# Which row of a step a token gets: ranks laid eight rows apart, in two mixture-of-experts stages

## The chip, the cores and the metric

The kernel runs on one core of one Trainium2 chip. The metric is device time in microseconds (us) of one execution. Median of three runs before the change: 1887.09 us (1879.42 to 1887.37).

## The reference, cut to what matters

Two transformer blocks over one sequence of 512 tokens with 1024 features, in float32. Each block mixes the tokens (attention and gated linear attention in the first, two attentions in the second) and then runs a mixture of experts. Only the latter is touched:

```python
# first block: 32 experts in 4 groups; each token takes the 2 best experts of its best group
hid = silu(h @ w_g[e]) * (h @ w_u[e]) * gate[:, e]      # w_g[e], w_u[e]: 1024 x 256
out = out + hid @ w_d[e]                                # w_d[e]: 256 x 1024
# second block: 64 experts in 8 groups; each token takes 6 experts out of its 4 best groups
xb = x_pad[tok]                                         # the tokens of expert e
hb = silu(xb @ w_exp_gate[e]) * (xb @ w_exp_up[e])
yb = (hb @ w_exp_down[e]) * g[:, None]
routed = segment_sum(yb, row_tok)                       # added back to each token's row
```

So 512 x 2 = 1024 (token, expert) pairs are computed in the first block and 512 x 6 = 3072 in the second. An expert's three weights are 1 MiB each, and all are read from HBM once: 96 MiB and 192 MiB.

## The kernel before, in words

Every expert stage works in steps of 128 rows, the partitions of an on-chip tile. A row of a step holds one token of one expert. A token's *rank* is its place among the tokens that chose the expert.

- First block, `paired_experts_stage`, 16 steps: expert `e` has rows 0 to 63 and expert `e + 8` rows 64 to 127.
- Second block, `sorted_experts_stage`, 39 steps. Experts 0 to 3 have a step each (WHOLE, 128 rows). The other sixty are sorted by their count on the chip; the ten largest get 128 rows each, the next fourteen 96 rows and share a step with one of the fourteen smallest in the other 32 (MIXED), and the twenty-two between pair up with 64 rows each (EVEN). `expert_steps` interleaves them.

For each step, VectorE compares each token's rank with a row of numbers, one for each row of the step (`onehot`, L1753 and L2083), TensorE multiplies this with the token numbers and gives a list: the token of each row, or a number past the end where a row has none. GpSimd issues an indirect DMA that gathers the listed rows of `h_scratch` (4 KB each) into the step's 128 rows (L1805, L2133), three steps ahead of their use. TensorE turns them (L1695, L2021), multiplies by gate and up weights (L1682, L2008), turns the hidden rows (L1670, L1996) and multiplies by the down weights (L1718, L2043). GpSimd then issues a second indirect DMA that adds the 128 result rows to the accumulator in HBM (`scatter_add`, L2329). Rows without a token are skipped by both.

Weights come by plain DMAs from SyncE's queue, 1 MiB each, over 128 partitions of 8 KB (L1608 and L1612 in the first block, L1554 to L1564 in the second). Their buffers are rings: in the first block the gate and up loads of pair p are issued once the gate and up products of pair p - 3 are done, the down loads of pair p - 1 once the down products of pair p - 3 are. SyncE issues in program order; an issue itself can take long when the queue is full. All DMAs, SyncE's and GpSimd's, run on the same 16 DMA engines.

The numbers that the ranks are compared with are, before, 0, 1, 2, ... (`K.iota`) in the first block and 1, 2, 3, ... (`order.places`, the last `held` of 1 to 128) in the second, where a slot with fewer rows has an offset added to its ranks. So rank n stands in row n of the expert's part of the step.

The routing and the ranks are made one stage earlier, in `output_and_ranks` of each block; VectorE there waits for the router's product before `vector(...)` (L1329).

Of the kernel before, what the change touches and what calls it, by code (L numbers as in the profile page):

```python
# [18 lines left out]
ALU = mybir.AluOpType  # L19
# [3 lines left out]
P = 128  # L23
S = 512
T = S // P
# [1152 lines left out]
def output_and_ranks(K, tag, preload, m, width, router, gate=None, gate_ready=None, vectors=(), gain=None,  # L1178
# [9 lines left out]
    load_router, load_next, scalar, vector = router  # L1188
# [6 lines left out]
    with nc.Block(no_gpsimd_drain=True) as block:  # L1195
# [101 lines left out]
        @block.vector  # L1297
        def _(dve):
            step = K.dve.on(dve)

            def add(u):
                j, t = divmod(u, T)
                x = K.x[:, t, 512 * j:512 * j + 512]
                dve.wait_ge(K.products, at_out[u])
                src = K.bank[u][:, :]
                if gate is not None:
                    step(dve.tensor_tensor(src, src, gate[:, 512 * j:512 * j + 512], ALU.mult))
                dve.tensor_tensor(x, x, src, ALU.add).then_inc(added, 1)

            weights.low(dve, 0)  # L1310
            weights.low(dve, 1)
            if gate is not None:
                dve.wait_ge(*gate_ready)
            for t in range(T):
                add(t)
            dve.wait_ge(*gain_ready)
            if scale is not None:
                step(dve.scalar_tensor_tensor(out=gain, in0=scale, scalar=1.0, in1=gain, op0=ALU.add, op1=ALU.mult))
            for t in range(T):
                add(T + t)  # L1320
                dve.wait_ge(std, t + 1)
                step(dve.reciprocal(rs[:, t:t + 1], sd[:, t:t + 1]))
                ins = dve.scalar_tensor_tensor(out=K.hr[:, t, :], in0=K.x[:, t, :], scalar=rs[:, t:t + 1], in1=gain,
                                               op0=ALU.mult, op1=ALU.mult)
                if shift is not None:
                    step(ins)
                    ins = dve.tensor_tensor(K.hr[:, t, :], K.hr[:, t, :], shift, ALU.add)
                ins.then_inc(normed, 1)
            dve.wait_ge(K.products, K.router_at)  # L1329
            vector(dve, step, K.bank[2][:, 0:T * width].rearrange("p (t n) -> p t n", t=T))  # L1330
            step(dve.tensor_copy(m.table[:, :, :, 1], m.gate))
            dve.tensor_copy(m.table[:, :, :, 0], K.token_id[:, :].unsqueeze(2).broadcast_to([P, T, E])).then_inc(chosen, 1)

            if shared:
                shared.vector(dve)
            for t in range(T):
                step(dve.memset(m.parts[:, t, :, 0], float(P * t - NO_TOKEN)))
            step(dve.tensor_scalar(m.parts[:, :, :, 1], K.token_id[:, 0:1].unsqueeze(2).broadcast_to([P, T, E]),
                                   float(NO_TOKEN), None, ALU.add))
            if order:  # L1340
                order.constants(dve, step)
                dve.wait_ge(K.products, at_rank[0])
                order.vector(dve, step)
                return
            step(dve.tensor_copy(m.parts[:, :, :, 2], m.gate))
            step(dve.tensor_tensor(m.rest, m.gate, m.parts[:, :, :, 2], ALU.subtract))
            step(dve.tensor_copy(m.parts[:, :, :, 3], m.rest))
            step(dve.tensor_tensor(m.rest, m.rest, m.parts[:, :, :, 3], ALU.subtract))
            step(dve.tensor_copy(m.parts[:, :, :, 4], m.rest))
            dve.wait_ge(K.products, at_rank[0])  # L1350

            step(dve.scalar_tensor_tensor(out=m.rank, in0=K.bank[3][:, 0:T * E].rearrange("p (t e) -> p t e", t=T),
                                          scalar=1.0, in1=m.chosen, op0=ALU.add, op1=ALU.mult))
            dve.tensor_scalar(m.rank, m.rank, -1.0, None, ALU.add).then_inc(tables, 1)
            dve.tensor_reduce(m.tiny[:, 0:1], K.bank[2][:, 0:E], AX.X, ALU.max).then_inc(tables, 1)
            dve.wait_ge(tables, 2)
            step(dve.tensor_copy(m.most, m.tiny[:, 0:1]))
# [50 lines left out]
QUARTER = P // 4  # L1408
# [16 lines left out]
    return steps  # L1425


def row_tiles(part):
    if part.stop - part.start in (QUARTER, 3 * QUARTER):
        return [slice(n, n + QUARTER) for n in range(part.start, part.stop, QUARTER)]  # L1430
    return [part]


class ExpertOrder:


    def __init__(self, K, m):
        s = K.sem
        self.K, self.m = K, m
        made, made_mm = s("order_tables_made"), s("order_products_made")  # L1440
        self.beats_ready, self.slots_ready, self.rank_ready, self.ids_ready, self.turned_copied = ((made, n) for n in range(1, 6))
        self.place_mm, self.ids_mm, self.turn_mm, self.slot_mm = ((made_mm, n) for n in range(1, 5))
        self.made, self.made_mm = made, made_mm
        f = K.heads
        self.key_base, self.key, self.beats, self.light, self.count = (f[:, 5120 + 64 * n:5184 + 64 * n] for n in range(5))
        self.junk, self.slots, self.turned = f[:, 5440:5568], f[:, 5568:5696], f[:, 5696:6208]
        self.own, self.beaten, self.slot, self.last, self.number = (f[:, 6208 + n:6209 + n] for n in range(5))
        self.places = K.small[:, 768:896]
        self.scatter_base = {EVEN: K.small[:, 896:897], MIXED: K.small[:, 897:898]}
        self.ids = K.small[0:1, 900:964].bitcast(I32)  # L1450
        flat = K.keep.rearrange("p t s -> p (t s)")
        self.both = flat[:, 512:1024].rearrange("p (t n) -> p t n", t=T)
        m.rank, m.gate = self.both[:, :, 0:64], self.both[:, :, 64:128]
        self.rank = m.chosen

    def constants(self, dve, step):
        K = self.K
        step(dve.tensor_scalar(self.key_base, K.iota[:, 0:64], -1.0, 63.0, ALU.mult, ALU.add))
        step(dve.tensor_scalar(self.key_base[:, 0:STATIC], K.iota[:, 0:STATIC], -FIXED, STATIC * FIXED, ALU.mult, ALU.add))
        step(dve.tensor_scalar(self.places, K.iota[:, :], 1.0, None, ALU.add))  # L1460
        step(dve.tensor_scalar(self.number, K.token_id[:, 0:1], float(NO_TOKEN), None, ALU.add))
        step(dve.tensor_scalar(self.last, self.number, 64.0, 64.0, ALU.is_ge, ALU.mult))
        step(dve.tensor_scalar(self.scatter_base[EVEN], self.last, float(S // 64), float(NO_TOKEN), ALU.mult, ALU.add))
        step(dve.tensor_scalar(self.own, self.number, float(3 * QUARTER), float(S), ALU.is_ge, ALU.mult))
        step(dve.tensor_scalar(self.scatter_base[MIXED], self.own, float(NO_TOKEN), None, ALU.add))
        step(dve.tensor_scalar(self.last, self.last, 63.0, None, ALU.add))
# [159 lines left out]
HALF = P // 2  # L1626


def paired_experts_stage(K, m, weights, next_vectors):
# [12 lines left out]
    onehot = f[:, 7680:8192].bitcast(BF16).rearrange("p (b t s) -> p b t s", b=2, t=T)  # L1642
# [17 lines left out]
    with nc.Block(no_gpsimd_drain=True) as block:  # L1660
# [64 lines left out]
        def _(dve):  # L1725
            for i in steps:
                if has(i, 0):
                    b, r = i % 2, i % 6
# [6 lines left out]
                if has(i, 1):  # L1735
                    b = (i + 1) % 2
# [4 lines left out]
                if has(i, 3):  # L1741
                    if i >= 3:
                        dve.wait_ge(scattered, 16 * (i - 2))
                    q = (i + 3) % 6
# [4 lines left out]
                if has(i, 4):  # L1749
                    b, e = i % 2, weights.pairs[i + 4][0]  # L1750
                    if i >= -2:
                        dve.wait_ge(list_mm, i + 3)
                    dve.tensor_tensor(onehot[:, b, :, :].rearrange("p t (n s) -> p t n s", n=2),  # L1753
                                      K.iota[:, 0:HALF].unsqueeze(1).unsqueeze(1).broadcast_to([P, T, 2, HALF]),
                                      m.rank[:, :, e:e + 9:8].unsqueeze(3).broadcast_to([P, T, 2, HALF]),
                                      ALU.is_equal).then_inc(listed, 1)
                if has(i, -1):
# [180 lines left out]
def sorted_experts_stage(K, m, weights, overflow, final):  # L1938
# [47 lines left out]
    with nc.Block(no_gpsimd_drain=True) as block:  # L1986
# [63 lines left out]
        def _(dve):  # L2050
            step = K.dve.on(dve)
            for i in steps:
# [24 lines left out]
                if has(i, 4):  # L2077
                    b = i % 2
                    if i >= -2:
                        dve.wait_ge(list_mm, i + 3)  # L2080
                    for slot, part in zip(steps_of[i + 4][0], ROWS[steps_of[i + 4][1]]):
                        held = part.stop - part.start
                        dve.tensor_tensor(onehot[:, b, :, part], order.places[:, P - held:P].unsqueeze(1).broadcast_to([P, T, held]),  # L2083
                                          order.rank[:, :, slot:slot + 1].broadcast_to([P, T, held]),
                                          ALU.is_equal).then_inc(listed, 1)
                if has(i, -1):
# [1184 lines left out]
```

## Time and profile before

| | |
|---|---|
| median of three runs | 1887.09 us (1879.42 to 1887.37) |
| the profiled execution, its own time | 1890.83 us |
| its span, first to last instruction | 1889.1 us |
| TensorE busy | 1655.1 us, 88% of the span |
| VectorE / ScalarE / GpSimd busy | 647.6 / 439.2 / 484.1 us |
| DMA of SyncE's queue (q1) | 411.13 MB, 56.3% of 16 engines' span |
| DMA of GpSimd's queue (q0) | 33.60 MB, 7.1% |
| first expert stage | about 429 to 712 us |
| second expert stage | about 1249 to 1860 us |

Busy TensorE is time with a matmul in flight; in a stage that waits for weights, the view of waits tells more. A DMA share is the mean over the core's 16 DMA engines; it can pass 1 by a little, since one packet's recorded time overlaps the next one's.

### The profile page before, as it was taken

Reading aid. Unit: us, or ns where it says so; the run is one execution under the profiler, and the core shown is the slowest. Engines: PE = TensorE matmul, PEld = TensorE weight load, DVE = VectorE, ACT = ScalarE, POOL = GpSimd, SP = SyncE. Lnnn points to the kernel's source line nnn. Section 1 sums busy time; section 2 is a strip of 40 time slices with the busy share of each in tenths; the row PEclk is TensorE's granted clock in tenths of the full one; section 3 lists DMA queues with packets and bytes.
Section 4 is the critical chain, followed back from the end, with each engine's and each line's share of the span. In section 5 each row is a group of like instructions: output and inputs, shape, how many; then the busy total and the mean of one; then the engine's idle time right before and its main releaser. Section 6 shows DMA issues by size and latency. Waiting matters only on the chain. (4 is left out here: it accounts for less than half of the span.)

```text
span 1889.1 us, 21925 instructions
## 1 busy us (share of the span) xinstructions
PE 1655.1 (88%) x7996; PEld 911.2 (48%) x7996; DVE 647.6 (34%) x1629; ACT 439.2 (23%) x945; POOL 484.1 (26%) x386
## 2 busy tenths in 40 slices
PE   6989999898999896999999969889997788887882
PEld 3334446773333334678678857544433333332330
DVE  1775515442111116662453244432222221221212
ACT  2411216421111014662453222111110000000001
POOL 4997907001111114760200000012221111111110
PEclk9799999988999997999999979979998898988996
DMA  5353320457999955422103335558999999999974
GB/s 200 134 178 123 134 89 5 176 204 300 402 407 404 401 199 182 157 89 90 51 1 101 120 143 212 228 197 310 391 394 392 376 374 369 373 372 364 366 281 160
DMA packets 110807, 446.23 MB, mean 236 GB/s; under 512 B 20356, under 2 KB 24852, under 8 KB 73320
## 3 DMA queue, kind: packets, MB, share of 16 engines
q1 hardware_dynamic: 94824, 411.13, 56.3%
q0 software_dynamic: 15840, 33.60, 7.1%
q8 instruction: 68, 1.11, 0.2%
q14 instruction: 43, 0.35, 0.1%
q10 hardware_dynamic: 32, 0.04, 0.0%
HBM read 427.33 MB, written 44.10 MB: 250 GB/s over the span
## 5 line engine op out<-in xcount | busy, mean ns | idle before, releaser
L2008 PE MATMUL bank<-big,heads 128*32 128x512 f32 (+2 forms) x1040 | 263.9, 669 | 47.7 <-DMA big<-in_w_exp_up_dram 31.9
L2008 PEld LDWEIGHTS bank<-big,heads 128*32 128x32 f32 (+2 forms) x1040 | 83.3, 140 | 173.8 <-issue 173.2
L2329 POOL DMA_INDIRECT acc_scratch<-heads,small x55 | 87.2, 1586 | 249.6 <-DVE heads L2093 143.7
L460 PE MATMUL bank<-big,h_cols 128*128 128x512 f32 x320 | 143.4, 603 | 0.3 <-ACT heads L610 0.3
L2059 DVE SCALAR_TENSOR_TENSOR heads<-heads,small,bank 128x256 f32<-128x256 f32 x39 | 18.7, 480 | 352.0 <-ACT heads L2111 352.0
L2133 POOL DMA_INDIRECT heads<-h_scratch,small x39 | 40.5, 1040 | 341.2 <-DVE small L2076 333.1
L1175 PE MATMUL bank<-causal,ident 128*128 128x512 f32 x174 | 90.2, 667 | 15.3 <-PEq L178 15.3
L2008 PE MATMUL bank<-junk_and_spare,heads 128*32 128x512 f32 (+2 forms) x272 | 84.9, 650 | 21.0 <-DMA big<-in_w_exp_up_dram 21.0
L818 POOL TENSOR_SCALAR junk_and_spare<-junk_and_spare,cond 128x512 f32<-128x512 f32 x56 | 97.5, 1742 | 5.5
L2111 ACT ACTIVATE heads<-bank 128x256 f32<-128x256 f32 x39 | 15.0, 384 | 359.0 <-PE bank L2008 359.0
L460 PEld LDWEIGHTS bank<-big,h_cols 128*128 128x128 f32 x320 | 60.0, 192 | 76.7 <-issue 76.2
L1114 PE MATMUL bank<-big_parts,x_res_parts 128*128 128x512 f32 x224 | 88.3, 394 | 0.0
L1682 PE MATMUL bank<-big,heads 128*64 128x512 f32 x352 | 82.3, 622 | 5.9 <-DMA big<-in_w_exp_up_dram 5.1
L2093 DVE TENSOR_TENSOR heads<-bank,gain 128x512 f32<-128x512 f32 x78 | 50.3, 686 | 103.3 <-PE bank L2043 103.3
L2008 PE MATMUL bank<-h_cols,heads 128*128 128x512 f32 (+2 forms) x160 | 76.9, 637 | 0.0
L821 POOL TENSOR_TENSOR h_rows<-h_rows,junk_and_spare 128x512 f32<-128x512 f32 x56 | 74.2, 1324 | 4.7
L3170 POOL TENSOR_TENSOR heads<-heads,gain 128x2048 f32<-128x2048 f32 x1 | 4.5, 4517 | 252.4 <-DMA shift<-in_g_final_dram 252.4
L1733 DVE SCALAR_TENSOR_TENSOR heads<-heads,small,bank 128x256 f32<-128x256 f32 x16 | 7.7, 481 | 176.1 <-ACT heads L1778 176.1
L1175 PEld LDWEIGHTS bank<-causal,ident 128*128 128x128 f32 x174 | 35.0, 211 | 65.7 <-issue 65.7
L1113 PE MATMUL bank<-big_parts,x_res_parts 128*128 128x512 f32 x160 | 63.5, 397 | 2.0 <-DVE big_parts L1098 2.0
L933 PE MATMUL bank<-heads,big 128*128 128x64 f32 x480 | 64.0, 266 | 0.6 <-DVE h_rows L997 0.4
L2043 PE MATMUL bank<-x_res,heads 128*32 128x512 f32 (+2 forms) x272 | 62.0, 596 | 1.1 <-DVE heads L2093 1.1
(475 smaller groups left out, 3241.6 us busy)
## 6 DMA issues: line engine op xcount, KB each, us to landing
big<-in_w_exp_gate_dram SPq DMA_DIRECT2D x65, 1024.0 KB, 16.9
big<-in_w_exp_up_dram SPq DMA_DIRECT2D x65, 1024.0 KB, 25.3
x_res<-in_w_exp_down_dram SPq DMA_DIRECT2D x38, 1024.0 KB, 28.7
h_rows<-in_w_exp_down_dram SPq DMA_DIRECT2D x28, 1024.0 KB, 29.7
big<-in_w_in_dram SPq DMA_DIRECT2D x13, 2048.0 KB, 9.0
junk_and_spare<-in_w_mod_dram SPq DMA_DIRECT2D x24, 1024.0 KB, 5.4
big<-in_w_exp_down_dram SPq DMA_DIRECT2D x19, 1024.0 KB, 26.8
junk_and_spare<-in_w_exp_gate_dram SPq DMA_DIRECT2D x16, 1024.0 KB, 19.0
```

The source lines that it names most:

```text
L460: mm = pe.matmul(out, lhsT, rhs, start=c == 0, stop=c == len(lhs_rhs) - 1)
L818: ins = pool.tensor_scalar(acc if first else w[:, c, :], w[:, c, :], cond, None, ALU.mult)
L821: ins = pool.tensor_tensor(acc, acc, w[:, c, :], ALU.add)
L933: mm = pe.matmul(K.bank[5 + u % 2][:, 0:64], turn[:, u % 3, P * k:P * k + P], K.v[:, k, 64 * h:64 * h + 64], start=k == 0, stop=k == t)
L1113: pe.matmul(banks[t][:, :], a_high, high, start=c == 0, stop=False)
L1114: pe.matmul(banks[t][:, :], a_high, low, start=False, stop=False)
L1175: pe.matmul(bank[:, :], K.ident[:, :], K.causal[:, :], start=True, stop=True)
L1682: mm = pe.matmul(b_au[b][part, :], xt[:, b, P * c + HALF * n:P * c + HALF * n + HALF], gu[places[n]][:, :, c, :], start=c == 0, stop=c == ...
L2008: mm = pe.matmul(b_au[b][tile, :], xt[:, b, P * c + tile.start:P * c + tile.stop], gu[places[n][0]][:, :, c, :], start=c == 0, stop=c == K ...
L2043: mm = pe.matmul(b_y[half][tile, :], hidt[:, b, P * j + tile.start:P * j + tile.stop], dn[places[n][0]][:, j, 512 * half:512 * half + 512] ...
L2093: dve.tensor_tensor(ys[:, b, cols], b_y[half][:, :], K.gain[:, cols], ALU.mult).then_inc(y_taken, 1)
L2329: return pool.indirect_dma_start(out=acc, out_offset=bass.IndirectOffsetOnAxis(at, 0), in_=rows, in_offset=None, bounds_check=acc.shape[0] ...
```

## The change

A new function makes the comparison numbers: row 8q + j of an expert's part (`held` rows, j from 0 to 7) gets j x (held / 8) + q. So consecutive ranks stand eight rows apart, and after held / 8 of them the next row of each group of eight is filled. The first block uses one such row of 64 numbers for both halves; the second keeps four, for 128, 96, 64 and 32 rows, each with the offset that its ranks carry. All are made in `output_and_ranks` before the wait for the router's product, and read by the comparisons in place of `K.iota` and `order.places`. Nothing else is changed.

```diff
                 ins.then_inc(normed, 1)
+            if order:
+                for held, out in order.places.items():
+                    ranks_of_rows(K, dve, step, out, P - held + 1)
+            else:
+                ranks_of_rows(K, dve, step, K.small[:, 1920:1984], 0)
             dve.wait_ge(K.products, K.router_at)
...
+def ranks_of_rows(K, dve, step, out, first):
+    held = out.shape[1]
+    by_engine = [P, held // 8, 8]
+    step(dve.scalar_tensor_tensor(out=out.rearrange("p (q j) -> p q j", j=8),
+                                  in0=K.iota[:, 0:8].unsqueeze(1).broadcast_to(by_engine), scalar=float(held // 8),
+                                  in1=K.iota[:, 0:held // 8].unsqueeze(2).broadcast_to(by_engine), op0=ALU.mult, op1=ALU.add))
+    if first:
+        step(dve.tensor_scalar(out, out, float(first), None, ALU.add))
...
-        self.places = K.small[:, 768:896]
+        self.places = {P: K.small[:, 1920:2048], 3 * QUARTER: K.small[:, 706:802], P // 2: K.small[:, 802:866],
+                       QUARTER: K.small[:, 964:996]}
...
-        step(dve.tensor_scalar(self.places, K.iota[:, :], 1.0, None, ALU.add))
...
-                                      K.iota[:, 0:HALF].unsqueeze(1).unsqueeze(1).broadcast_to([P, T, 2, HALF]),
+                                      K.small[:, 1920:1984].unsqueeze(1).unsqueeze(1).broadcast_to([P, T, 2, HALF]),
...
-                        dve.tensor_tensor(onehot[:, b, :, part], order.places[:, P - held:P].unsqueeze(1).broadcast_to([P, T, held]),
+                        dve.tensor_tensor(onehot[:, b, :, part], order.places[held].unsqueeze(1).broadcast_to([P, T, held]),
```

## Rows read from the trace of the kernel before

**Rows 1.** Windows, both expert stages: start and end, length, busy us, clock, DMA share, GB/s.

```profile
core 0: us, PE busy (x) PEld busy (x) DVE busy (x) ACT busy (x) POOL busy (x), PEclk, DMA share, GB/s
449.00:459.00 10.00, 9.83 (x58) 4.49 (x56) 1.97 (x5) 1.37 (x3) 0.99 (x1) 1.00 0.57 213
459.00:469.00 10.00, 10.00 (x53) 4.12 (x48) 2.66 (x6) 1.58 (x3) 1.51 (x2) 1.00 0.82 311
500.00:640.00 140.00, 136.64 (x633) 55.12 (x632) 21.28 (x48) 16.29 (x34) 22.45 (x17) 0.99 1.02 404
1400.00:1600.00 200.00, 162.23 (x932) 66.45 (x930) 41.74 (x104) 16.39 (x36) 31.57 (x24) 0.90 1.01 378
```

**Rows 2.** Waits of TensorE, 440 to 700 us: total, times, longest.

```profile
PE bank L1682 <- DMA big<-in_w_exp_up_dram: 5.1, 2, 4.3
PE bank L1695 <- DMA heads<-h_scratch,small: 3.6, 1, 3.6
PE bank L1682 <- DMA junk_and_spare<-in_w_exp_up_dram: 2.4, 1, 2.4
```

**Rows 3.** Waits of TensorE, 1300 to 1840 us.

```profile
PE bank L2008 <- DMA big<-in_w_exp_up_dram: 52.9, 12, 6.7
PE bank L2008 <- DMA h_cols<-in_w_exp_up_dram: 13.0, 4, 4.0
PE bank L2043 <- DMA heads<-in_w_exp_down_dram: 5.6, 3, 2.0
...
PE bank L2043 <- DMA h_rows<-in_w_exp_down_dram: 3.1, 1, 3.1
```

**Rows 4.** DMA queues, 500 to 640 us: packets, MB, share of 16 engines.

```profile
q1 hardware_dynamic: 7083, 51.59, 88.0%
q0 software_dynamic: 2590, 4.89, 13.5%
```

**Rows 5.** DMA queues, 1400 to 1800 us.

```profile
q1 hardware_dynamic: 18204, 132.55, 83.3%
q0 software_dynamic: 7058, 16.46, 16.1%
```

**Rows 6.** Source line L1612 (down loads) at 482, 560 and 681 us: issue, then issue to landing.

```profile
L1612 SPq DMA_DIRECT2D x_res<-in_w_exp_down_dram x2: 328/380/433, 482.5 to 482.9; - x2
...
DMA to landing us min/median/max: 10.7/11.7/12.8
...
L1612 SPq DMA_DIRECT2D big<-in_w_exp_down_dram x1: 328/328/328, 560.9 to 560.9; - x1
...
DMA to landing us min/median/max: 19.7/21.1/22.6
...
L1612 SPq DMA_DIRECT2D x_res<-in_w_exp_down_dram x2: 328/380/432, 681.7 to 682.1; - x2
...
DMA to landing us min/median/max: 13.1/14.1/15.1
```

**Rows 7.** DMA packets, 459.9 to 461.74 us, then 461.74 to 463.6 us.

```profile
DMA packets 140, 0.78 MB, mean 425 GB/s; under 512 B 17, under 2 KB 17, under 8 KB 72
q0 software_dynamic: 65, 0.23, 30.0%
...
DMA packets 190, 0.79 MB, mean 427 GB/s; under 512 B 91, under 2 KB 91, under 8 KB 95
q0 software_dynamic: 79, 0.02, 4.4%
```

**Rows 8.** Waits of SyncE's queue, 1390 to 1800 us.

```profile
SPq L1564 <- PE bank L2043: 5.5, 3, 2.2
SPq L1554 <- PE bank L2008: 2.9, 2, 2.5
```

**Rows 9.** Timeline of VectorE ahead of each router: start, us, idle before and its end.

```profile
403.02 0.16 DVE L1322 RECIPROCAL small<-small 128x1 f32<-128x1 f32 x1 [1.54 <-ACT small L1272]
...
413.80 0.31 DVE L1905 TENSOR_TENSOR small<-bank,small 128x144 f32<-128x144 f32 x1 [9.29 <-PE bank L1222]
...
1202.91 0.43 DVE L3070 TENSOR_TENSOR keep_mask<-keep_mask,small 128x256 f32<-128x256 f32 x1 [15.60 <-ACT keep_mask L3064]
```

**Rows 10.** Timeline of SyncE's queue, from 594 us.

```profile
594.27 8.81 SPq L1608 DMA_DIRECT2D big<-in_w_exp_gate_dram  x1
```

## The prediction

> **What bounds the kernel now.** I read the windows of both expert stages first, then what TensorE waits for, then the DMA queues. In the first stage TensorE is busy 136.6 of 140 us and all 16 DMA engines are full too (share 1.02) [rows 1]. TensorE waits for weights only 7.5 us there [rows 2]: it sets the pace, with weights close behind. In the second stage it waits some 75 us for weights [rows 3], the DMA share is 1.01 [rows 1], and SyncE's queue waits only 8.4 us in 410 for a buffer that TensorE has to free [rows 8]: that stage goes at the pace of the DMAs.
>
> So the question is how much work the busiest of the 16 DMA engines has. A weight load gives all 16 the same. The gathers and scatter-adds don't: only rows that hold a token move 4 KB, so an engine's work depends on which rows it serves.
>
> **Prices.** Between 500 and 640 us q1 took 88.0% of 16 x 140 us for 51.59 MB, 38.2 us of engine time per MB; q0 took 13.5% for 4.89 MB, 1194 packets of 4 KB, 0.253 us each [rows 4]. The shares sum to 1.017, since records overlap; divided by that, an expert's three weights (3.146 MB) cost every engine 7.4 us, a step of two experts 14.8 us, and a token 0.25 us for its gather and 0.25 us for its scatter.
>
> **Which engine serves which row.** This decides the sign, and three rules are at hand: eight neighbouring rows to an engine (under which the change spreads the tokens evenly), row modulo 16, or groups of four. I take the gather of pair 3: the reference's routing gives its experts 34 and 25 tokens, rows 0 to 33 and 64 to 88. An engine alternates a gathered row with a weight packet, one turn each 0.46 us. In the first four turns (1.84 us) the packets between 512 B and 8 KB, which are the gathered rows, number 72 - 17 = 55, in the next four turns 95 - 91 = 4 [rows 7]. With eight rows to an engine nine engines would carry them, at most 36 in four turns. With row modulo 16 the first four turns would cover rows 0 to 63, 34 of them filled, and the other 25 would follow. Groups of four give this picture: nearly all engines have four filled rows and then empty ones. The single packet records behind these rows, which no view lists, follow engine by engine: seven engines with 4 tokens and one with 6, six with 4, one with 1, one with none. That is engine = (row / 4) modulo 8, plus 8 for rows from 64 on; an engine has rows 4e to 4e + 3 and the four that lie 32 further.
>
> [...]
>
> **Tokens per engine.** The change fills rows 8q + j with small j first, and j < 4 always falls to an even engine. With counts from the reference's routing I laid out each step by that map.
> - First stage, before, engines 0 to 15: 102 86 75 66 64 63 56 52 79 66 64 64 64 60 39 24. After: 124 24 123 22 123 15 121 12 116 6 113 6 108 4 106 1. An expert with up to 32 tokens used eight engines four deep; now it uses four engines eight deep. The busiest engine goes from 102 to 124.
> - Second stage, before: 304 304 304 299 282 261 250 236 195 164 133 102 82 67 49 40. After: 302 142 301 140 301 130 301 123 282 65 280 62 274 52 270 47. The busiest engine stays: from the fifth step on engine 0 has 8 tokens in every step, before and after, 280 in all.
>
> **Check of the model on before.** First stage: an expert pair takes TensorE 15.7 us. From 482.5 to 560.9 us, five steps, the slower down load's time to landing grows from 12.8 to 22.6 us [rows 6], 1.96 us a step, so the engine it waits for needs 17.6 us a step: 14.8 for weights and 2.8 for 5.7 tokens. The map gives engine 0 6.3 in steps 3 to 8; the mean over the engines is 4, eight neighbouring rows would give 8. Second stage, 1400 to 1800 us: 132.55 MB at 38.2 / 1.017 us is 311 us per engine; 16.46 MB are 2009 tokens, 25.5 steps of 78.8, so 204 for engine 0, 102 us [rows 5]. Sum 413 of 400 us, full within the error of the prices; the mean engine has 63 us of rows, 374 in all.
>
> **The change, first stage.** While DMA engines still had gaps (share 0.57 and 0.82 up to 469 us [rows 1]) extra rows cost nothing. Afterwards engine 0 is busy without a gap. Extra tokens on it: gathers of steps 3 to 15, 2 2 3 2 0 0 0 0 1 3 4 0 0, sum 17; scatters of steps 0 to 12, ahead of the last gate and up loads, 18. 35 x 0.25 = 8.7 us. Can slack hide it? TensorE already waits for late weights at the stage's end [rows 2] and a load is by then issued against a full queue (8.81 us for one issue [rows 10]), so I count all of it. Bounds: 3 us, if the lateness of the loads (22.6 us and growing) can still rise by some us before TensorE feels it; 11 us, for all 22 tokens at 0.5, plus 0.5 us for step 1's gather, which TensorE waits for at the start [rows 2]. I take 8.5, near the end that the full queue speaks for. The last down load lands in 13 to 15 us [rows 6] and moves as a whole; the last scatter has eight tokens on engine 0 either way.
>
> **Second stage.** Busiest engine 280 against 280 where it binds; the two tokens less lie in the steps before. 0, bounds -1 (2 x 0.5) and +3, if eight engines near the top instead of four make the slowest one a little later.
>
> **VectorE.** One added instruction in the first block, eight in the second less one removed, on 32 to 128 columns; the nearest rows are 0.16 us (1 column) and 0.31 us (144) [rows 9], so at most 0.3 and 2.2 us. They stand before a wait that lasts 9.29 and 15.60 us [rows 9], which hides them; without that cover they would cost these 2.5 us. No engine gets a new wait. The comparisons keep shape and type and only read another tile: 0. Nothing else is moved, on no queue.
>
> **Sum.** 1890.8 (the profiled execution's own time) + 8.5 = 1899.3. That execution lies 3.7 us above the median of 1887.1; on the median it is 1895.6. 0.5%, 9.4 us, is about what a measurement of this kernel can tell from no change, so the forecast, +0.45%, lies at the upper edge of it.
>
> **Rivals.**
> - *Faster: an engine serves eight neighbouring rows.* Then the first stage's 7.5 us of waits go, and the second's busiest engine falls from 312 tokens to 228: 84 x 0.5 = 42 us, less than the 75 of waits. 1887.1 - 49 = 1838. Against it: 55 rows in four turns [rows 7] where it allows 36, and 5.7 tokens a step where it gives 8. Chance 0.06.
> - *No change: the first stage has room.* TensorE waits only 7.5 us in 260; if that comes from single late loads rather than the queue, most extra rows are hidden, +0 to +4: 1889. For it: waits at few places, the longest 4.3 us [rows 2]. Against: landing times grow step by step [rows 6]. Chance 0.28.
> - *Slower by more: engine e and e + 8 share something.* Before, a full engine (304) faced a light one (195); after it is 302 with 282. If a pair's work counts together, 85 tokens more at half of 0.5 are 21 us in the second stage, with the first stage 1917. It decides once both are busy together. Against it: packets cost no more with all 16 full (share 1.02 at 404 GB/s [rows 1]). Chance 0.05.
> - A small gain by luck of order, to -10 us, since the light engines now hold fewer rows and stay out of the way: 0.05.
>
> **Chances and range.** The forecast has 0.56, its own range 1890 to 1900. Within 0.5% (1877.7 to 1896.5): 0.32 of it, most of the second rival, in all 0.55. Slower: 0.24 of it, the third rival and a little of the second, 0.33. Faster 0.12. The range 1881 to 1905 leaves out the first and third rivals.
>
> **What would show it.** In the first stage the down loads' time to landing should grow by 2.5 to 3 us a step instead of 1.96, reach 25 us or more at 561 us, and TensorE's waits for weights rise from 7.5 to some 16 us; the stage ends 8 us later. In the second stage, length and waits stay within 3 us. VectorE's new instructions show no row that anyone waits for. Wrong would be: the stages' lengths unchanged with TensorE's waits equal (room after all), or the second stage shorter by tens of us (the map is eight neighbouring rows).

## The result, and the profile after

The changed kernel takes 1900.2 us (median of five runs, 1898.12 to 1903.63), the one before 1887.1: ratio 1.0069, 95% interval 1.0051 to 1.0086, so 10 to 16 us slower. A second comparison gave 1.0062 (1.0048 to 1.0075). One of the 23 runs of the kernel before that stood beside the first experiments took 2775.31 us at a granted clock of 0.55; the ratios leave it out. The profiled executions differ by 7.3 us of span (1889.1 and 1896.4). I give each stage a length of its own, from GpSimd's memset at its start to the issue of its last scatter; the parts outside the expert stages differ from one execution to the next (1001.4 us before, 998.0 and 1000.3 us in two of the changed kernel), while these two lengths repeat within 3 us, the first within 0.5.

Windows over exactly these stretches, of the changed kernel and of the one before (start and end, length, busy us of each engine, granted clock, DMA share, GB/s):

```profile
427.00:714.95 287.95, 262.56 (x1186) 106.88 (x1186) 42.82 (x96) 32.65 (x65) 42.62 (x33) 0.96 0.91 346
1257.28:1867.72 610.44, 514.09 (x2972) 215.56 (x2972) 135.64 (x337) 53.18 (x117) 102.51 (x79) 0.92 0.94 349
```

```profile
428.91:705.79 276.88, 261.15 (x1186) 105.37 (x1186) 42.83 (x96) 32.69 (x65) 42.67 (x32) 0.97 0.92 360
1248.81:1859.61 610.80, 517.13 (x2972) 216.48 (x2972) 135.61 (x337) 53.27 (x117) 102.67 (x79) 0.92 0.93 349
```

The first stage grew by 11.1 us, the second by nothing. TensorE's waits for weights in the first, of the changed kernel, 436 to 720 us (total, times, longest), sum to 16.0 us, where [rows 2] has 7.5:

```profile
PE bank L1698 <- DMA big<-in_w_exp_up_dram: 11.0, 4, 4.6
PE bank L1698 <- DMA junk_and_spare<-in_w_exp_up_dram: 5.0, 2, 4.4
PE bank L1711 <- DMA heads<-h_scratch,small: 3.8, 1, 3.8
```

The down loads (L1628 now) at 481 us, and those at 559 us, five steps on, answer to [rows 6]:

```profile
L1628 SPq DMA_DIRECT2D x_res<-in_w_exp_down_dram x2: 328/380/433, 480.9 to 481.3; - x2
...
DMA to landing us min/median/max: 12.2/13.3/14.3
...
L1628 SPq DMA_DIRECT2D big<-in_w_exp_down_dram x1: 328/328/328, 559.3 to 559.3; - x1
...
DMA to landing us min/median/max: 28.6/29.7/30.7
```

The slower of two took 14.3 us at 481 us and 30.7 us at 559 us. So the time to landing grows by 3.3 us a step instead of 1.96, and it has reached 30 us when the first wait for a weight comes, at 564 us.

The gather of pair 3, again 34 and 25 tokens, now in turns of the same length as [rows 7], 458.20 to 460.05 us and then to 461.90:

```profile
DMA packets 156, 0.77 MB, mean 416 GB/s; under 512 B 47, under 2 KB 47, under 8 KB 77
...
DMA packets 161, 0.78 MB, mean 421 GB/s; under 512 B 52, under 2 KB 52, under 8 KB 80
```

77 - 47 = 30 rows in the first four turns and 80 - 52 = 28 in the next four. Before they were 55 and 4. The map gives 31 and 28: in all, four engines have eight rows each, four have six or seven, eight have at most one. The order that is to spread an expert's tokens has gathered them on half of the engines.

### The profile page after: what moved, and what is told of

It reads as the page before. It is cut to its first block and busy times, and to the rows that moved or that the text cites. A ratio compares the mean times of both kernels' runs of the same rounds, so it can differ in the third digit from the quotient of the medians.

```text
span 1896.4 us, 21934 instructions
## 1 busy us (share of the span) xinstructions
PE 1650.0 (87%) x7996; PEld 909.7 (48%) x7996; DVE 646.5 (34%) x1637; ACT 439.1 (23%) x945; POOL 482.6 (25%) x386
## 5 line engine op out<-in xcount | busy, mean ns | idle before, releaser
L460 PEld LDWEIGHTS bank<-big,h_cols 128*128 128x128 f32 x320 | 60.3, 193 | 77.2 <-issue 76.7
L1115 PE MATMUL bank<-big_parts,h_cols_parts 128*128 128x512 f32 x160 | 62.9, 393 | 0.0
```

The source lines that it names most:

```text
L460: mm = pe.matmul(out, lhsT, rhs, start=c == 0, stop=c == len(lhs_rhs) - 1)
L1115: mm = pe.matmul(banks[t][:, :], a_low, high, start=False, stop=c == n - 1)
```

## The experiments

"First" and "second" are the lengths of the stages as above; "busiest" is the number of tokens that the map of groups of four gives the busiest engine. Each ratio is to runs of the kernel before made beside it, whose median was 1887.1, 1887.9 or 1887.7 us; the stage lengths are of one profiled execution each.

| kernel | median us | ratio to before, 95% | first (busiest) | second (busiest) |
|---|---|---|---|---|
| before | 1887.1 | | 276.9 (102) | 610.8 (304) |
| after | 1900.2 | 1.0051 to 1.0086 | 288.0 (124) | 610.4 (302) |
| the change, first block only | 1901.2 | 1.0058 to 1.0090 | 287.8 (124) | 610.8 (304) |
| the change, second block only | 1889.4 | 0.9995 to 1.0021 | 277.3 (102) | 612.2 (302) |
| its instructions, old order | 1885.5 | 0.9981 to 1.0012 | 276.9 (102) | 610.9 (304) |
| rows backwards | 1874.6 | 0.9924 to 0.9951 | 277.5 (102) | 596.4 (277) |
| balanced, first block only | 1879.5 | 0.9951 to 0.9978 | 268.3 (79) | 610.4 (304) |
| balanced | 1838.1 | 0.9708 to 0.9748 | 268.7 (79) | 572.4 (211) |
| balanced, snake | 1836.1 | 0.9715 to 0.9741 | 269.0 (76) | 568.2 (198) |

**The change in one block at a time.** First block only, against the kernel before:

```diff
+            if not order:
+                ranks_of_rows(K, dve, step, K.small[:, 1920:1984], 0)
...
-                                      K.iota[:, 0:HALF].unsqueeze(1)...
+                                      K.small[:, 1920:1984].unsqueeze(1)...
```

> The change in the first block alone; the second keeps ranks one behind the other. Theory (the busiest DMA engine sets the end; 102 tokens become 124 in the first stage, 304 stay 302 in the second): all of the change's loss is here, +8 to +13 us against the kernel before, TensorE's waits for weights in the first stage 16 us instead of 7.5. Rival (even engines full in both stages hurt, the second too): +4 to +7 us here and the rest in the second block alone.

Second block only, the other part of the diff:

> The change in the second block alone. Theory: 0, within 3 us of the kernel before, since engine 0 has 280 tokens from the fifth step on in either order; last scatter minus first gather of the second stage 608 us as before. Rival (eight engines near the top instead of four, or a pair e and e + 8 sharing something): +5 to +20 us.

The whole loss is the first block's: 1901.2 against 1887.9 us in those runs, first stage +10.9 us, waits for weights 15.7 us. The second block's part is 1.0008, no change that can be told; its stage measured 612.2 us, 1.4 longer, in a single execution, and the changed kernel's, with the same order there, 610.4 and 609.6 us. With eight engines near the top instead of four nothing is lost, so the rival that engines e and e + 8 share something has fallen: it wanted 21 us.

**The same instructions, the old order.**

```diff
-                                  in0=K.iota[:, 0:8].unsqueeze(1).broadcast_to(by_engine), scalar=float(held // 8),
-                                  in1=K.iota[:, 0:held // 8].unsqueeze(2).broadcast_to(by_engine), op0=ALU.mult, op1=ALU.add))
+                                  in0=K.iota[:, 0:held // 8].unsqueeze(2).broadcast_to(by_engine), scalar=8.0,
+                                  in1=K.iota[:, 0:8].unsqueeze(1).broadcast_to(by_engine), op0=ALU.mult, op1=ALU.add))
```

> All of the change's instructions and tiles, but the numbers they make are 8q + j for row 8q + j: ranks one behind the other, as before. Theory: 0, within 2 us of before. Rival (the added VectorE work, or the new places of the numbers, cost the part of the loss that the first stage's waits don't explain): +3 to +6 us.

0.9996 (0.9981 to 1.0012), and both stages as before to 0.1 us. VectorE's added work costs nothing that can be seen: the timeline of the changed kernel has the instructions (start, us) right behind the last norm, and the last of the eight ends 13.7 us before VectorE's next one. The first two of them:

```profile
1194.53 1.22 DVE L1327 TENSOR_TENSOR h_rows<-h_rows,shift 128x1024 f32<-128x1024 f32 x1
1195.67 0.28 DVE L1437 SCALAR_TENSOR_TENSOR small<-iota 128x128 f32<-128x128 f32 x1
1195.99 0.23 DVE L1441 TENSOR_SCALAR small<-small 128x128 f32<-128x128 f32 x1
```

**Ranks spread by the map of groups of four.** If the reason is right, the change's aim can be had with other numbers. Row 4e + b of each block of 32 rows gets start + stride x b + e:

```diff
+    base = {P: [(16, 0), (16, 64), (16, 8), (16, 72)], 96: [(16, 0), (8, 64), (16, 8)], 64: [(8, 0), (8, 32)], 32: [(8, 0)]}[held]
+    for n, (stride, start) in enumerate(base):
+        block = out[:, 32 * n:32 * n + 32]
+        step(dve.scalar_tensor_tensor(out=block.rearrange("p (e b) -> p e b", b=4),
+                                      in0=K.iota[:, 0:4].unsqueeze(1).broadcast_to([P, 8, 4]), scalar=float(stride),
+                                      in1=K.iota[:, 0:8].unsqueeze(2).broadcast_to([P, 8, 4]), op0=ALU.mult, op1=ALU.add))
+        if start + first:
+            step(dve.tensor_scalar(block, block, float(start + first), None, ALU.add))
```

> In both blocks ranks laid so that consecutive ones fall to different engines under the map of groups of four (row 32a + 4e + b of a half holds rank 32a + 8b + e, and so on for 128, 96 and 32 rows); 10 + 1 more short instructions on VectorE. By the map the busiest engine has 79 tokens instead of 102 in the first stage and 211 instead of 304 in the second. Theory: the first stage loses its 7.5 us of waits, the second up to 93 x 0.5 = 46 us of its 76: faster than before by 40 to 55 us, about 1840. Rival (eight neighbouring rows to an engine): this order would be no better than that of the change, within 5 us of it or slower. Rival (the total over all engines bounds, not the busiest): no change, within 3 us of before.

1838.1 us, ratio 0.9728: 50 us less than before and 62 less than the change. Neither rival allowed that. Windows of its two stages, and TensorE's waits for weights in the first:

```profile
426.80:695.52 268.72, 257.50 (x1186) 103.99 (x1186) 42.84 (x96) 32.64 (x65) 42.61 (x32) 0.98 0.95 371
1239.90:1812.30 572.40, 502.82 (x2972) 212.12 (x2972) 135.64 (x337) 53.18 (x117) 102.50 (x79) 0.95 0.96 372
```

```profile
PE bank L1700 <- DMA big<-in_w_exp_up_dram: 2.5, 2, 1.8
PE bank L1700 <- DMA junk_and_spare<-in_w_exp_up_dram: 0.8, 1, 0.8
```

The total was as expected, its parts were not. The first stage lost 8.2 us, but only 4.2 of them are waits for weights (7.5 before, 3.3 now). The second lost 38.4 us, not 46: its waits for weights fell by 23.1 us (from 76.7 to 53.6 between 1300 and 1860 us), and TensorE's busy time by 14.3 us (517.13 to 502.82). Why busy time falls too is said below, with the first stage's. One reason for the smaller gain can be read before 1400 us, where TensorE hardly waits, so that tokens taken off a DMA engine there save little; this is the kernel before:

```profile
1300.00:1400.00 100.00, 98.61 (x609) 41.85 (x609) 27.87 (x70) 10.92 (x24) 22.15 (x17) 1.00 0.99 375
```

The second stage moves 372 GB/s instead of 349, with the same bytes. That before, the light engines were held up while one had a long queue, is an estimate of mine and was not shown; no view shows single engines.

> The balanced order in the first block alone, busiest engine 79 tokens instead of 102. Theory: the first stage shortens as in the kernel balanced in both, from 277 to 269 us, the second stays 611: -8 us, 1880. With the change's 124 this gives three points for the first stage. Rival (gains of the two stages depend on each other): less than 5 or more than 12 us.

In the first block alone, the helper as above and the diff of the first-only kernel: 1879.5 us, first stage 268.3. The first stage's gain doesn't depend on the order in the second; the balanced order in the second block alone was not run.

**Which engine, or how full.** The rows run backwards:

```diff
+    step(dve.tensor_scalar(out, K.iota[:, 0:held], -1.0, float(held - 1 + first), ALU.mult, ALU.add))
```

> Rank n of an expert in the last row but n of its part, in both blocks. By the map this gives the busiest engine 102 tokens in the first stage, as before, but engine 7 instead of 0, and 277 in the second (engine 15) instead of 304. Theory: first stage as long as before, within 1.5 us (277 us from its memset to its last scatter issue), second shorter by 27 x 0.5 = 13 us (598 instead of 611): 1874. Rival (it matters which engines are full, not how full the fullest is, for example if 7 and 15 are slower ones): first stage longer by 3 us or more, second not shorter.

```profile
428.60:706.11 277.51, 260.99 (x1186) 105.36 (x1186) 42.83 (x96) 32.65 (x65) 42.60 (x32) 0.97 0.92 359
1246.57:1842.96 596.39, 504.92 (x2972) 214.69 (x2972) 135.61 (x337) 53.18 (x117) 102.51 (x78) 0.94 0.94 357
```

1874.6 us. With the full engine at the other end of the row the first stage is unchanged, and the second is 14.4 us shorter for 27 tokens less, 0.53 us each (expected 0.5). It is the fill of the fullest engine, not its number, that counts. This is also the plainest reading of the second stage before: every step has an expert's part that starts at row 0 and fills from below, which by the map piles up on engines 0 to 3 (the parts from row 64 or 96 on begin at engine 8), and counting backwards takes 27 of 304 off the fullest.

**How far it goes.** The second rounds of the 128-row and 64-row parts run backwards over the engines (`K.desc` counts down):

```diff
+    base = {P: [(16, 0, 0), (16, 72, 1), (16, 8, 0), (16, 64, 1)], 96: [(16, 0, 0), (8, 64, 0), (16, 8, 0)],
+            64: [(8, 0, 0), (8, 32, 1)], 32: [(8, 0, 0)]}[held]
...
+        engine = K.desc[:, 0:8] if back else K.iota[:, 0:8]
...
```

> The balanced order with the second rounds of the 128-row and 64-row parts running backwards over the engines, so that the same engines don't always get the odd tokens: busiest engine 76 instead of 79 in the first stage, 198 instead of 211 in the second (mean 192). Theory: 1 us in the first and up to 13 x 0.5 = 6.5 us in the second against balanced: 1830 to 1835. Rival (balanced is already held by something else, TensorE's own pace or the total over all engines): within 2 us of balanced, 1838.

A miss: 1836.1 us (1834.06 to 1838.58), within noise of balanced (both 0.9728), and 1.9 us below it, where the rival stands. The second stage is 4.2 us shorter in the profiled execution, not 6.5, and one execution can be off by nearly as much; the first not at all. A window inside the second stage, of the balanced kernel, answers to the last line of [rows 1]:

```profile
1400.00:1600.00 200.00, 166.02 (x1007) 68.75 (x1007) 45.28 (x114) 17.73 (x39) 35.21 (x27) 0.94 1.02 399
```

Here the share of 1.02 goes with 399 GB/s, near the first stage's 404, and hardly a packet is drawn out (the last section). So I take all 16 engines to be full, with the mean load of 192 tokens as the limit, and 198 or 211 on the fullest no longer matters much. No run here tells this apart from other limits, such as TensorE's own pace.

**The changed kernel again.**

> The changed kernel once more, beside the others on one chip: both theories +11 to +13 us against before, first stage 288 us from memset to last scatter issue.

1899.4 us, ratio 1.0062, first stage 288.0 us, second 609.6.

## Why the prediction held, and where it was short

- *What bounds the kernel*: right for the first stage and, from about 1400 us on, for the second; ahead of that the second goes at TensorE's pace (98.61 of 100 us busy). The second stage follows its busiest DMA engine: 302 or 304 tokens give 609.6 to 612.2 us in seven executions, 277 give 596.4, 211 give 572.4, though the last 66 tokens bring only 0.36 us each. The first stage is TensorE's with weights close behind: 79, 102 and 124 tokens give 268.7, 276.9 and 288.0.
- *The map of rows to engines*: right, and it decided the sign. The turns of one gather in the changed kernel are 30 and 28 rows where it gives 31 and 28, and the orders made for it are the fastest; the packet records of both gathers, below, show it engine by engine. The rival of eight neighbouring rows, which would have given 1838 for the change, is out; that its number is the time of the balanced kernel is partly chance. Both price an even spread, but the rival took 7.5 and 42 us from waits alone, and the balanced kernel lost 8.2 and 38.4 us in the two stages, part of it as busy time, and the rest of its 50 elsewhere.
- *Second stage 0*: right.
- *VectorE hidden*: right (0.9996 with the same instructions).
- *Room in the first stage*: none, so the second rival (no change, 0.28) is out; the small gain from lighter engines (0.05) didn't come either. Waits for weights rose from 7.5 to 16.0 us, by 8.5; the step's 35 x 0.25 = 8.7 us stands. As for the full queue: before the change, between 453 and 667 us, no issue of a load took over 1.65 us with fewer than eight earlier loads still to land, and every one that took longer, up to the 8.81 us of [rows 10], began with 8 to 11 of them still to land.
- *The sum, +8.5 us*: too small, and this term, the first stage's, is where. It measured +11.1 us (10.9 and 11.1 in the two other kernels with that order). TensorE's idle time grew by 9.7 (25.4 against 15.7): 8.5 for weights, 0.9 ahead of a down product late in the stage, 0.3 at the start. And its busy time grew by 1.4 us for the same 1186 matmuls, at a mean granted clock of 0.96 instead of 0.97. The sum had only the waits in it and put this loss at nothing; it is what the granted clock costs behind a wait, as shown below this list. At 11.1 us the stage meets the upper bound I gave, 11 us and 0.5, which is chance: that bound priced 22 tokens at 0.5 us and no loss of clock. On the median, the forecast of 0.45% became 0.69%, beyond what I had called the likeliest class (within 0.5%, 0.55); the chance of slower was 0.33.
- *Growth of the landing time*: forecast 2.5 to 3 us a step, measured 3.3. The map gives engine 0 at most 8 tokens a step, 14.8 + 4.0 = 18.8 us, a growth of 3.1; the rest is within the error of the prices.

**What a wait costs beyond its length.** Behind its longest waits in these runs TensorE ran at a granted clock of 0.50 for 3.4 us. The timeline of the changed kernel has 32 gate and up matmuls behind a wait of 3.52 us and as many behind one of 0.76 us; the window (columns as in [rows 1]) is the stretch at the lower clock in the first group:

```profile
582.95 8.78 PE L1698 MATMUL bank<-big,heads 128*64 128x512 f32 x32 [3.52 <-DMA big<-in_w_exp_up_dram]
...
601.16 7.09 PE L1698 MATMUL bank<-big,heads 128*64 128x512 f32 x32 [0.76 <-DMA big<-in_w_exp_up_dram]
```

```profile
583.40:586.80 3.40, 3.40 (x10) 1.21 (x8) 0.00 (x0) 0.00 (x0) 0.00 (x0) 0.50 0.83 228
```

The same work takes 8.78 instead of 7.09 us: 3.4 us at a granted clock of 0.50 cost 1.7 us. From 450 us to the end of the first stage the changed kernel has three such stretches, at 583.4, 620.9 and 658.5 us, each in or right behind one of its three longest waits (3.5, 4.4 and 4.6 us). The kernel before has two, at 615.9 and 653.4 us, right behind waits of 2.4 and 4.3 us. The balanced kernel has none: its longest wait for a weight is 1.8 us, and from 450 to 680 us its granted clock is 1.00. One stretch more is up to 1.7 us, and the busy time grew by 1.4; two fewer are 3.4 us, and it fell by 3.65. Not every wait brings such a stretch: none lies behind the one of 2.1 us that ends at 693.7 us in the changed kernel.

**The map, engine by engine.** The single packet records don't name their engine, but they tell the engines apart: from 459.9 to 463.6 us of the kernel before, each packet begins 3 or 4 ns ahead of the end of another, which makes 16 chains, with packets of both queues in each. A gathered row (0.16 us) and a weight packet (0.31 us) take turns in a chain, 0.46 us together. Thirteen chains have 4 gathered rows, one has 6, one has 1 and one none. That is what groups of four, eight engines to a half, give for 34 and 25 tokens, when row 32 begins again at the half's first engine. In the changed kernel, from 458.2 to 462.5 us, the map gives 8 rows on four engines, 7 on one, 6 on three, 1 on two and none on six. The chains have just that, but for two with 3 and 5 rows, which are 8 and none if they are crossed where packets of both begin within 1 ns. A load of weights does give all engines the same: from 453.2 to 459.9 us of the kernel before every chain has eight weight packets, then one of 4 bytes, then weight packets again. For the scatters too the map fits: of the 58 rows of the first pair's scatter, 51 began within four turns of 0.64 us before the change and 36 after it, by the single packet records of the traces, and the map puts 55 and 31 in the first four rows of each engine. The stage lengths of all the orders tried, which depend on gathers and scatters alike, agree.

What stays open: the 2 us between the first stage's +11.1 and the median's +13.1 lie inside the interval (10 to 16 us), and I didn't try to settle them. The price of a token does split by the packet records: between 500 and 640 us of the kernel before, 600 packets of 4 KB took 0.16 us on the mean and 593 took 0.33 us. The packets of pair 3's gather took the former and those of the first pair's scatter the latter. So a gathered row costs about 0.16 us and a scattered one 0.33 us, not 0.25 each. The term of 17 gathers and 18 scatters comes to 8.7 us all the same.

## What to carry to other kernels

When rows move by indirect DMA and only some rows are filled, count the filled rows per DMA engine, not per step: the fullest engine sets when loads land that share it, and a mean DMA share near 1 hides this (here 124 instead of 102 tokens on it made the time to landing grow by 3.3 instead of 1.96 us a step, and between 1400 and 1600 us of the kernel before the share was 1.01, in a stage with 304 tokens on the fullest engine and 192 on the mean one). Read the map off one gather in the trace before choosing an order; here groups of four rows, 32 apart, and an order made for groups of eight made it worse where one made for groups of four took off 50 us. Where TensorE sets the pace, cost a wait of some us above its length: here up to 1.7 us more, for 3.4 us at a granted clock of 0.50.

## What the runs showed that I had not expected

A share of 1.01 in the windows of the kernel before [rows 1] looked like full engines; yet the same bytes went through 6% faster once spread (378 to 399 GB/s between 1400 and 1600 us, at a share of 1.02). A packet's recorded time is then no proof of work. The single packet records show where the time is: an 8 KB weight packet took 0.31 us in the median in both, but in that window of the kernel before 197 of 8151 took over 0.4 us, up to 2.4 us, and what they took beyond 0.31 us is 3.7% of the 16 engines' time; in the balanced kernel 11 of 8598 did. The first stage shows the same between 500 and 640 us: 12 such packets of 6298 before, at 404 GB/s, and 178 of 5988 in the changed kernel, at 383. On which engines they lie, and what held them up, no run here shows. And the granted clock followed the waits: 0.96, 0.97 and 0.98 in the first stage with 16.0, 7.5 and 3.3 us of waits for weights.
